# State-space heads in two groups of eight, started beside the last dense unit, with a one-pass spreading product and GpSimd at work

## The reference

```
xbc = silu(causal_dwconv(xbc, conv_w) + conv_b)        # 1536 channels: 1024 values, 256 B, 256 C
dt  = softplus(dt_raw + dt_bias);  a = -exp(a_log)
acs = cumsum(dt * a) within each chunk, per head
within a chunk:  y[t] = sum_{s<=t} exp(acs[t]-acs[s]) * (C[t].B[s]) * dt[s] * x[s]
state of a chunk = sum_s B[s] * exp(acs[last]-acs[s]) * dt[s] * x[s],  decayed and carried to the next
from before it:  y[t] += exp(acs[t]) * C[t] . state;   y += d_skip * x;   y = norm(y * silu(z))
```

## Time and profile before

| | us |
|---|---|
| median of 3 runs | 2396.05 |
| lowest, highest | 2395.46, 2401.61 |
| span of the profiled execution | 2395.9 |
| PE busy in it | 2264.7 |
| DVE, ACT, POOL busy | 1237.3, 808.8, 380.6 |

### The profile page before, as it was taken

How to read it: one execution, slowest core, us unless ns; L and a number is a source line. 1 busy time by engine, 2 the same in 40 slices (tenths; PEclk the granted TensorE clock), 3 DMA queues, 4 the chain that set the end, 5 groups by cost and what they waited for, 6 DMA issues and landing times.

```text
span 2395.9 us, 34312 instructions
## 1 busy us (share of the span) xinstructions
PE 2264.7 (95%) x14568; PEld 1645.9 (69%) x14568; DVE 1237.3 (52%) x1625; ACT 808.8 (34%) x1201; POOL 380.6 (16%) x265
## 2 busy tenths in 40 slices
PE   8999998997789989999999999999999999999998
PEld 5677885322223327877677699899787668989976
DVE  5885654300000007365765498486463749938745
ACT  3533232111011105123452354243342836514424
POOL 1001001100001000000000154252100024605310
PEclk9999999999999999999999999999999999999999
DMA  7223316999999993222111123333222012233330
GB/s 297 72 87 120 125 71 281 397 420 420 419 417 420 420 383 157 89 96 80 36 56 68 55 96 102 105 104 107 112 89 87 1 53 80 95 108 106 108 112 36
DMA packets 59020, 388.76 MB, mean 162 GB/s; under 512 B 7739, under 2 KB 7867, under 8 KB 17008
## 3 DMA queue, kind: packets, MB, share of 16 engines
q1 hardware_dynamic: 52896, 375.29, 40.9%
q0 software_dynamic: 5104, 8.09, 0.9%
q10 hardware_dynamic: 864, 3.15, 0.4%
HBM read 383.13 MB, written 13.63 MB: 166 GB/s over the span
## 4 chain that ended last, share of the span: by engine, by line
PE 79%; DMA 10%; DVE 5%; ACT 3%; SPq 1%; issue 1%; POOL 0%; DVEq 0%; POOLq 0%; ACTq 0%
PE psD L3570 38%; PE psD L2656 8%; PE psA L2656 8%; DMA ring<-w_moe 8%; PE psD L1424 7%; PE psA L3570 3%; DMA arena<-w_moe 1%; PE psA L1424 1%; SPq L804 1%; PE psA L2640 1%; DVE ring_r L3169 1%; PE psA L3645 1%; ACT ring_r L2951 1%; PE psA L3862 1%; PE psA L3802 1%
## 5 line engine op out<-in xcount | busy, mean ns | idle before, releaser
L3570 PE MATMUL psD<-rounded,ring_r 128*128 128x512 f32 (+1 forms) x3192 | 759.3, 398 | 6.8 <-DVE ring_r L3169 3.3
L3570 PEld LDWEIGHTS psD<-rounded,ring_r 128*128 128x128 f32 (+1 forms) x3192 | 594.6, 187 | 166.9 <-issue 16.5
L1424 PE MATMUL psD<-ring,arena 128*32 128x512 f32 x1568 | 177.2, 594 | 30.7 <-DMA ring<-w_moe 30.2
L3169 DVE TENSOR_TENSOR ring_r<-ring,ring_r 128x2048 fp32r<-128x2048 f32 (+2 forms) x71 | 158.9, 2238 | 81.7 <-ACT ring_r L2951 79.7
L2656 PE MATMUL psD<-rounded,fast_r 128*128 128x256 f32 x1680 | 200.0, 279 | 0.0
L2656 PE MATMUL psA<-rounded,fast_r 128*128 128x256 f32 x1680 | 199.8, 279 | 0.0
L1424 PE MATMUL psD<-arena 128*32 128x512 f32 x1504 | 173.5, 602 | 27.1 <-DMA arena<-w_moe 25.0
L2656 PEld LDWEIGHTS psA<-rounded,fast_r 128*128 128x128 f32 x1680 | 198.2, 188 | 0.4
L2656 PEld LDWEIGHTS psD<-rounded,fast_r 128*128 128x128 f32 x1680 | 198.1, 188 | 0.1
L2951 ACT ACTIVATE ring_r<-ring 128x2048 fp32r<-128x2048 f32 (+2 forms) x71 | 131.8, 1856 | 192.6 <-PE psD L3570 172.7
L3570 PE MATMUL psD<-rounded,fast_r 128*128 128x512 f32 x792 | 185.4, 395 | 0.0
(11 more groups left out here) (552 smaller groups left out, 2738.5 us busy)
## 6 DMA issues: line engine op xcount, KB each, us to landing
ring<-w_dense SPq DMA_DIRECT2D x134, 1024.0 KB, 4.9
ring<-w_moe SPq DMA_DIRECT2D x49, 2048.0 KB, 34.0
arena<-w_moe SPq DMA_DIRECT2D x47, 2048.0 KB, 33.4
ring<-w_dense SPq DMA_DIRECT2D x16, 768.0 KB, 4.2
ring<-w_dense SPq DMA_DIRECT2D x16, 640.0 KB, 3.9
arena<-pair_rows SPq DMA_DIRECT2D x8, 512.0 KB, 8.0
arena<-x_t SPq DMA_DIRECT2D x1, 2048.0 KB, 8.0
token_rows<-arena ACTq DMA_DIRECT2D x4, 512.0 KB, 11.0
```

Of the source, the lines that this page charges most:

```text
L1424: mm = pe.matmul(bank_[32 * g:32 * g + 32], rows(g), weights(g), start=start, stop=stop_)
L3169: dve.tensor_tensor(lo_, src, hi, ALU.subtract).then_inc(sem("w_lo"), 1)
L3570: mm = pe.matmul(out, w[a], x[b], start=start and i == 0, stop=stop_ and i == 2)
```

## The change

The order of the xbc groups becomes 4, 5, 0, 1, 2, 3. The B transposes and the B-C products move up between the third and the fourth group, with ACT's copies and DVE's masking behind tile 1, the last of the third group. The first four spreads are issued before ("z", 0), and ACT and DVE begin the first two pairs of heads once their own convolution work is done. Values, states and carries are done per group of eight heads: group 0 before the third pair, group 1's values before it too, its states after the fifth pair. The spreading product reads 48 rows of fp32r (the rounded decays, zeros, the remainder) in place of 16 of fp32. GpSimd takes CE times C of the odd heads and the row scaling of the second group. The products of a pair alternate between the two heads. Both `keep_clock` calls of the stage and the early load of the exponent table are gone. Unchanged lines are left out of the diff at "...".

```diff
+XBC_ORDER = (4, 5, 0, 1, 2, 3)
+XBC_TILES = [2 * j + b for j in XBC_ORDER for b in range(2)]
...
-    a += [("bct", c) for c in range(4)] + [("xst", c, h) for c in range(4) for h in range(2)]
-    a += [("cb", g) for g in range(2)]
-    a += [("stt", c, g) for c in range(3) for g in range(2)]
-    a += [("acs", h) for h in range(16)]
+    a += [("bct", c) for c in range(4)] + [("cb", g) for g in range(2)] + [("acs", h) for h in range(4)]
+    a += [("xst", c, 0) for c in range(4)] + [("stt", c, 0) for c in range(3)] + [("xst", c, 1) for c in range(4)]
+    a += [("acs", h) for h in range(4, 10)] + [("stt", c, 1) for c in range(3)] + [("acs", h) for h in range(10, 16)]
...
-        X0_P = parts(14336, 27648, 8)
+        X0_P = parts(14336, 18432, 8)
...
-        DT = [flat(21504 + 512 * i, 512) for i in range(8)]
-        SELH = flat(21504, 2048).rearrange("p (h t) -> p h t", h=16)
+        DT = [flat(27648 + 512 * i, 512) for i in range(8)]
+        SELH = area_r(22528, 4).rearrange("p k t -> p (k t)").rearrange("p (h t) -> p h t", h=16)
+        ACS_P = area_r(24576, 1)[:, 0, :]
         GB = [flat(25600 + 512 * i, 512) for i in range(4)]
...
-        XDE = [flat(lo, 1024) for lo in (31744, 23552)]
+        XDE_TILE = [flat(lo, 512) for lo in (21504, 22016, 31744, 32256)]
+
+        def xde(c, g):
+            return XDE_TILE[c if g == 0 else (3, 0, 1)[c]]
...
+            def odd_head(h):
+                pool.wait_ge(sem("seg_exp"), h)
+                pool.tensor_tensor(CE[h % 4], CE[h % 4], BC[:, 2 + h // 8, :], ALU.mult).then_inc(sem("head_ce"), 1)
+
+            odd_head(1)
+            odd_head(3)
+            last = ("xst", 3, 1)
+            pool.wait_ge(freed(last), AUX_NO[last] // 4 + 1)
+            ready(pool, ("stt", 2, 0))
+            for c in range(3):
+                pool.tensor_tensor(xde(c, 1).rearrange("p (h v) -> p h v", h=8),
+                                   XDT[:, c, 512:1024].rearrange("p (h v) -> p h v", h=8),
+                                   dee[:, c, 8:16].unsqueeze(2).to_broadcast([P, 8, HD]), ALU.mult).then_inc(sem("xde"), 1)
+            for h in range(5, 16, 2):
+                odd_head(h)
...
-            for q in range(12):
+            for i, q in enumerate(XBC_TILES):
...
-            for c in range(4):
-                n_ = ("bct", c)
-                ready(act, n_)
-                act.activation(BTOK[:, c].rearrange("p g n -> p (g n)"), bank(n_)[:, 0:256], ACT.Copy)\
-                   .then_inc(freed(n_), 1)
-            for g in range(2):
+                if q == 1:
+                    for c in range(4):
+                        n_ = ("bct", c)
+                        ready(act, n_)
+                        act.activation(BTOK[:, c].rearrange("p g n -> p (g n)"), bank(n_)[:, 0:256], ACT.Copy)\
+                           .then_inc(freed(n_), 1)
+
+            def first_state(g):
                 n_ = ("stt", 0, g)
                 ready(act, n_)
                 act.activation(HIN[0][:, 512 * g:512 * g + 512], bank(n_), ACT.Copy).then_inc(freed(n_), 1)
-            step(act.activation(CE[3][:, 0:1], DTT[:, 0:1], ACT.Exp))
 
             def odd_head(h):
...
+                if h == 2:
+                    first_state(0)
+                if h == 8:
+                    first_state(1)
...
-                step(dve.tensor_copy(SELH[0:16], ident[0:16, 0:16].unsqueeze(2).to_broadcast([16, 16, P])))
+                step(dve.tensor_copy(SELH[0:32], ident[0:32, 0:16].unsqueeze(2).to_broadcast([32, 16, P])))
+                step(dve.tensor_copy(SELH[32:48], ident[32:48, 32:48].unsqueeze(2).to_broadcast([16, 16, P])))
+                step(dve.tensor_scalar(ACS_P[0:32], reset[0:32, :], 0.0, None, ALU.mult))
+                step(dve.tensor_copy(ACS_P[0:16], acs))
+                step(dve.tensor_tensor(ACS_P[32:48], acs, ACS_P[0:16], ALU.subtract))
...
+                if q == 1:
+                    for n in range(2):
+                        n_ = ("cb", n)
+                        ready(dve, n_)
+                        take(n_, dve.tensor_tensor(CBM[n].rearrange("p (c t) -> p c t", c=4),
+                                                   bank(n_).rearrange("p (c t) -> p c t", c=4),
+                                                   pair[:, 1, :].unsqueeze(1).to_broadcast([P, 4, P]), ALU.mult))
+            dve.wait_ge(sem("last_exp"), 2)
...
+            def values(g):
+                for c in range(4):
+                    n_ = ("xst", c, g)
...
-            def scaled_rows(c):
-                if c == 2:
-                    ready(dve, ("stt", 0, 1))
-                dve.tensor_tensor(XDE[c % 2].rearrange("p (h v) -> p h v", h=16),
-                                  XDT[:, c, :].rearrange("p (h v) -> p h v", h=16),
-                                  dee[:, c, :].unsqueeze(2).to_broadcast([P, 16, HD]), ALU.mult)\
-                   .then_inc(sem("xde"), 1)
...
+            def states(g):
+                hs_ = slice(512 * g, 512 * g + 512)
+                first = ("stt", 0, g)
+                dve.wait_ge(freed(first), AUX_NO[first] // 4 + 1)
...
                 dve.wait_ge(sem("seg_exp"), h if h % 2 == 1 else h + 2)
-                dve.tensor_tensor(CE[h % 4], CE[h % 4], BC[:, 2 + h // 8, :], ALU.mult).then_inc(sem("head_ce"), 1)
+                if h % 2 == 0:
+                    step(dve.tensor_tensor(CE[h % 4], CE[h % 4], BC[:, 2 + h // 8, :], ALU.mult))
                 dve.tensor_tensor(GB[h % 4], GB[h % 4], CBM[h // 8], ALU.mult).then_inc(sem("head_g"), 1)
 
-            for h in range(0, 16, 2):
+            def head_pair(h):
                 head_start(h)
                 head_end(h + 1)
                 head_end(h)
-                if h >= 2:
-                    head_out(h // 2 - 1)
+
+            head_pair(0)
+            head_pair(2)
+            values(0)
+            for c in range(3):
+                dve.tensor_tensor(xde(c, 0).rearrange("p (h v) -> p h v", h=8),
+                                  XDT[:, c, 0:512].rearrange("p (h v) -> p h v", h=8),
+                                  dee[:, c, 0:8].unsqueeze(2).to_broadcast([P, 8, HD]), ALU.mult).then_inc(sem("xde"), 1)
+            states(0)
+            values(1)
+            for h in range(4, 16, 2):
+                head_pair(h)
+                if h == 4:
+                    head_out(0)
+                if h == 8:
+                    states(1)
+                head_out(h // 2 - 1)
             head_out(7)
...
-            for j in range(6):
+            for j in XBC_ORDER[0:3]:
                 dense(("xbc", j), xr)
-            dense(("z", 0), xr)
-            pe.wait_ge(sem("xbc_done"), 12)
+            pe.wait_ge(sem("xbc_done"), 4)
             for c in range(4):
                 out = aux(("bct", c))
                 for g in range(2):
                     mm = pe.transpose(out[:, P * g:P * g + P], BC[:, g, P * c:P * c + P], ident)
                 filled(mm)
-            for c in range(4):
-                for h in range(2):
-                    out = aux(("xst", c, h))
-                    for k in range(4):
-                        mm = pe.transpose(out[:, P * k:P * k + P], YS2[:, 4 * h + k, P * c:P * c + P], ident)
-                    filled(mm)
             for g in range(2):
                 out = aux(("cb", g))
                 for c in range(4):
                     cs = slice(P * c, P * c + P)
                     mm = pe.matmul(out[:, cs], BC[:, g, cs], BC[:, 2 + g, cs], start=True, stop=True)
                 filled(mm)
-            for c in range(4):
-                n_ = ("bct", c)
-                pe.wait_ge(freed(n_), AUX_NO[n_] // 4 + 1)
-
-            def chunk_states(c):
-                pe.wait_ge(sem("xde"), c + 1)
-                for g in range(2):
-                    filled(pe.matmul(aux(("stt", c, g)), BTOK[:, c, g, :], XDE[c % 2][:, 512 * g:512 * g + 512],
-                                     start=True, stop=True))
-
-            pe.wait_ge(group_freed(("xbc", 5)), GROUP_NO[("xbc", 5)] // 2 + 1)
-            keep_clock(YD[0], 2)
-            for c in range(3):
-                chunk_states(c)
+            for j in XBC_ORDER[3:6]:
+                dense(("xbc", j), xr)
 
             def spread(h):
-                filled(pe.matmul(aux(("acs", h)), SELH[0:16, h, :], DT[7][0:16, :], start=True, stop=True))
+                filled(pe.matmul(aux(("acs", h)), SELH[0:48, h, :], ACS_P[0:48], start=True, stop=True))
+
+            def rows_of(g):
+                for c in range(4):
+                    out = aux(("xst", c, g))
+                    for k in range(4):
+                        mm = pe.transpose(out[:, P * k:P * k + P], YS2[:, 4 * g + k, P * c:P * c + P], ident)
+                    filled(mm)
+
+            def chunk_states(g):
+                if g == 0:
+                    for c in range(4):
+                        n_ = ("bct", c)
+                        pe.wait_ge(freed(n_), AUX_NO[n_] // 4 + 1)
+                for c in range(3):
```

(98 more changed lines are left out.)

5 lines of the change are left out of this document (1 added, 4 removed).

## The result

Over 6 runs each the kernel after took 2409.3 us in the median (2406.3 to 2413.3) and the one before 2397.5 (2395.5 to 2401.6): ratio 1.0039, 95% interval 1.0029 to 1.0049. It is slower: the ratio stands for 9.3 us, the two medians are 11.8 apart. The profiled spans are 2407.6 and 2395.9, 11.7 apart.

What follows compares the result with a forecast made beforehand. PE was taken to bound the kernel, busy 95% with 79% of the chain. 14.4 us lost up to the last xbc product, 4.0 won after, 0.6 clock: 11.0 on 2395.9, predicted 2407, 8-in-10 range 2398 to 2414.

Steps and rivals of the forecast that it cites:

- The stall at the B-C products: Before the first B-C product: PE waits 9.2 us for ACT's copy of the B transpose holding its bank.
- Clock behind the gap: After PE's stall at the B-C products: half-speed clock costs 2.55 us, bounds 0 to 5.1.
- ("z", 0) hides hardly a pair: Behind the last xbc product: ("z", 0) covers the last group's convolution and cuts, 11.7 us, and hardly any heads.
- Pairs 0 and 1: First two pairs of heads, with nothing running ahead: 8.3 us.
- First states and carries: After group 0's values and the scalings: first state product, copy and two carries, 3.2 us.
- Pair 2: Third pair, waiting for free banks, ACT's odd head and GpSimd's scalings before its CE: 7.5 us.
- Pair 3 with two head_outs, pair 4, states of the second group: Middle of the heads, where DVE paces the loop: 5.1, 4.5 and 2.9 us.
- Pairs 5, 6, 7: Last three pairs, GpSimd in the way at 5 and 7, ACT's cut at 7: 5.4, 4.5 and 6.0 us.
- The last product at low clock: Pair 7's product before ("z", 1), alternating heads at half speed: 3.1 us.
- The second part as a whole: From the last xbc product to ("z", 1): 71.9 us in place of 75.9, 4.0 won.
- the heavier rival: Heads: alternation gives nothing, clock stays low, 4.5 us per product, 4.9 more, 2.55 at ("z", 1); 2414 us, chance 0.14.
- the lighter one: Second part: no hold by GpSimd and full clock, last product ends 6.2 us earlier; 2401 us, chance 0.21.

Runs made afterwards that it cites:

- e1: Changed kernel with the B-C products and DVE's masking one xbc group later; 2399.1 us, 0.9998 of the kernel before.
- e4: Changed kernel with the old spreading product, 16 rows of fp32, without the operations building its 48 rows; 2413.8 us, 1.0054 of the kernel before.
- e7: e6 with 14 idle products put in PE's waits; 2393.0 us, 0.9973 of the kernel before.
- e3: Changed kernel with the two heads of a pair multiplied one after the other again; 2413.9 us, 1.0057 of the kernel before.
- e6: Changed kernel with B-C products one group later, the ("z", 1) cut behind early pairs, CE times C back on DVE; 2393.3 us, 0.9969 of before.
- f1: Kernel before with only the one-pass spread and the alternation of heads added; 2395.6 us, 0.9980 of the kernel before.
- after_again: The changed kernel run once more, unaltered, beside other runs; 2408.8 us, 1.0042 of the kernel before.

## Why the prediction was right

By its own steps, each with the forecast first:

- **The stall at the B-C products**: 9.2, measured 8.87. Cause as named, ACT's copy behind the cut; e1 takes it away. Transposes and B-C products moved in front: 2.65 forecast, 0.87 + 1.78 in e1's chain.
- **Clock behind the gap**: 2.55, measured 3.52 - 1.78 = 1.74. The low stretch was 3.1 us here and 5.1 in the row I took it from the earlier trace rows. The term was over by 0.8 in this trace (e4, with the same gap, had a low stretch of 6.2), and with 0.3 of the stall it makes the last xbc product 13.4 later where I had 14.4.
- **("z", 0) hides hardly a pair**: DVE began pair 0 at 1165.10, 11.7 after the last xbc product (1153.44), as forecast; ("z", 0), started at about 1154, has no longer than the 11.4 of a group.
- **Pairs 0 and 1**: 8.3, measured 1173.39 - 1165.10 = 8.3. Values and scalings 4.7, measured 4.8.
- **First states and carries**: 3.2, measured 5.3 (1178.2 to 1183.5). Here a term was under by 2.1. The state products ran at half speed, six in 5.46 us, because PE had waited for DVE before them; e7, with idle products in that wait, has them at full speed in 2.74. I had put the low clock at the last product only.
- **Pair 2**: 7.5, measured 6.2 (1186.5 to 1192.71).
- **Pair 3 with two head_outs, pair 4, states of the second group**: 5.1, 4.5 and 2.9; measured 5.2, 4.5 and 3.0.
- **Pairs 5, 6, 7**: 5.4, 4.5 and 6.0, measured 4.5, 4.5 and 5.7. GpSimd's hold cost time at pairs 0, 2 and 7. At pair 5 it was there too (one operation of DVE took 1.04 in place of 0.69), but in front of a wait for ACT. It cost 0.5 + 0.7 + 0.7 = 1.9 in place of 3.1.
- **The last product at low clock**: 3.1, measured 2.9. The low clock reached ("z", 1) and cost 1.6 there in this execution, 0 in the next; I took 0.6.

The rows for pair 7, its hold, the last product and the idle products before ("z", 1) in the kernel after:

```profile
1217.22 1.77 POOL L1761 TENSOR_TENSOR arena<-arena 128x512 f32<-128x512 f32 x1 [5.07 <-ACT arena L1850]
1218.17 1.36 DVE L2233 TENSOR_TENSOR arena<-arena 128x512 f32<-128x512 f32 x1 [0.31 <-ACT arena L1857]
1220.40 0.79 PE L2603 MATMUL psD<-arena 128*64 128x128 f32 x8 [3.90 <-DVE arena L2234]
1223.37 0.75 DVE L2217 SCALAR_TENSOR_TENSOR arena<-arena,par,psD 128x512 f32<-128x512 f32 x1 [2.45 <-PE psD L2610]
1224.17 2.07 PE L3633 MATMUL psD<-masks 128*128 128x512 f32 x2 [0.84 <-DVE arena L2217]
```

The second part as a whole came to the 4.0 that was forecast, but through errors of opposite sign: +2.1 for the states, -1.3 at pair 2, -1.2 from 5 to 7. (Taken to the first dense product of ("z", 1), where the forecast ended that part, 3.1 was won, 1226.24 - 1153.44 = 72.8 against 75.9; the other 0.9 is the low clock, which the sums here have in the last term.) So did the sum: 14.4 - 4.0 + 0.6 = 11.0 forecast, 13.4 - 4.0 + 1.6 = 11.0 measured. The mechanisms were right; that the total matches to a tenth is luck. The exclusive lock of the Trainium skill (SBUF — State Buffer, SBUF: two separate sides) is borne out where the two engines met (DVE 0.69 to 1.37). So is what the Trainium skill (TensorEngine Tiling (Array Packing), Key Properties) says of different tiles working in parallel (2.82 to 1.68 a pair). The rival without alternation had 4.5 for the last product, which e3 shows.

Three things in the working don't add up, without moving the forecast. The small operations of DVE come to 1.2 + 3 x 0.7 = 3.3 us and not 2.9; the 5.6 of cover hold for both, and the first tap came no later (1082.2 against 1083.4). The 4.9 us of the heavier rival and the 6.2 of the lighter one are not derived there; e3, which is the heavier rival's missing alternation alone, had 5.0. And the instruction of 1404.59 is a TENSOR_TENSOR, not a copy. The estimate that the spreads are nearly free stays open: 0.9 to 1.0 us in e4's heads, 2.9 by the ratios, which don't tell it from nothing.

Of the change's parts, read from the runs: the one wait at the B-C products costs about 10, the cut in front of the heads 2 to 4, CE on GpSimd about 2 (1.5 and 1.8 in the medians, 1.5 and 3.6 in the heads); alternation gives 4 to 5 inside the new order and the one-pass spread about 1 in the heads there, the two together 3 to 5 in the old one. The regrouping can pay only once the wait and the cut are out of its way, and that it then does is not shown: e6 against f1 has 175.3 against 179.8 in the stage, but ratios of 0.9969 and 0.9980 with overlapping intervals, on two chips. The dropped early load of the exponent table, on e6's path with 1.28 us, was not tried by itself.

## What to carry to other kernels

Before moving a small product up in PE's list, ask which bank it takes and where its last reader stands in that engine's list: a copy of 0.28 us, behind a group's convolution and a 1.9 us weight cut, held PE for 8.87. Moving it ahead of the cut alone could have saved at most the 1.9. Give work to a slower engine only where the faster one has no wait to fill with it, and look at whether the two meet in the same operations. When several engines take turns, change one list at a time: the gain of one part (4 to 5 us of alternation) and the loss of another (10 of a wait) are both invisible in the sum.

## What the runs showed that I had not expected

- After 8.87 us of idle time PE stood at 0.50 for 3.1 us; after 4.04 or more in the kernel before it was 5.1. A longer gap did not mean a longer low stretch. And the same gap did not always give the same stretch: 2.9 us in after_again, 6.2 in e4, both after 8.87 or 8.88.
- The low clock also came without such a gap, after waits of 3.3 and 3.7 us with little work between (the state products at 1177.2), and with idle products there it came at a later place in the one trace of e7.
- The fall at ("z", 1) comes in some executions of the same program and not in others (52.6 and 51.0), while the product before it was at 0.50 in both.
